# A mixture-of-experts step: x and h turned by VectorE in 32x32 blocks, x in its own column order, down loaded as gate, the bias in one step

## The chip, the cores and the metric

One core of a Trainium2 chip runs the whole program. The metric is the device time of one execution in microseconds, as the median of several runs.

## The reference

One layer of an encoder for 256 prompt frames and 64 sample frames, D_MODEL = 1024, all in float32: one input projection, band attention and a convolution branch, their mix, a LayerNorm, and then a mixture of 32 experts with the best 4 for each frame. The part that matters here is the last:

```python
logits = x @ w_router + b_router
top_val, top_idx = lax.top_k(logits, 4)
gate = softmax(top_val)
# for each frame and each of its 4 experts e
gt = minimum(x @ w_gate[e] + b_gate[e], 7.0)
up = clip(x @ w_up[e] + b_up[e], -7.0, 7.0)
h = gt * sigmoid(1.702 * gt) * (up + 1.0)
y += gate * (h @ w_down[e] + b_down[e])
# then
x = layer_norm(alpha * x + y) * g + b
```

Each expert's w_gate, w_up and w_down has 1024 x 1024 floats (4.19 MB); the 96 matrices are 403 MB.

## The kernel before

The program is written per engine, with semaphores. Ahead of the expert loop stand the projections, attention, convolution, the output projection and the first LayerNorm (`norm1`, `norm1_small`), then the router (`logits`, `largest`, `shares`, `ranked`), which leaves for each frame its rank within each expert and tables with the order of the experts.

**Blocks.** An expert's frames are cut into blocks of 32 slots. All in all there are 58 blocks; the 32 experts, in the order in which they are worked (order comes from `above_at`: one with many frames, then two with few), take 1, 1, 1, 7, 1, 1, 4, 1, 1, 4, 1, 1, 4, 1, 1, 3, 1, 1, 3, 1, 1, 3, 1, 1, 2, 1, 1, 2, 2, 2, 2, 1 blocks here.

**One block on TensorE.** PSUM rows are used as four strips of 32: strip q holds the 32 slots and the columns 256q to 256q + 255. In order: `gate_or_up` for gate (32 steps: 8 chunks of the 1024 inputs by 4 strips, each as two instructions, since float32; then the bias), `combine(i, 0)` of the block before, `gate_or_up` for up, `combine(i, 1)`, `gather` (the next block's rows of x, by the selection matrix `sel`), two transposes of `tin` that turn h, two small matmuls that spread the slot row of the next block (`who`, waited for under `bc_mm`), `combine(i, 2)`, two transposes that turn the gathered x (`turn_x`), and down (32 steps). `combine` sends the finished y of the block before back to the frames: tile 0 and 1 into PSUM banks 4 to 7, tile 2 into banks 4 and 5, and so each waits until VectorE has added what lay there (`yadd`).

**Turning.** Matmuls need x and h with the 1024 inputs on partitions. ScalarE copies the gathered rows from PSUM bank 2 to `tin` (`gathered`), TensorE turns 128 x 128 squares into bank 3, ScalarE copies them to `xg` (`turned`). h is computed by VectorE in `tin`, turned in the same way, and copied to `hT`. For this to give the rows that gate and up expect (partition p holds rows 8p to 8p + 7 of w_gate, 32 KB in one run), LayerNorm writes x in another column order: in `norm1` and `norm1_small` the writes are rearranged from (q c) to (c q), and the router's weights are loaded to match. w_down is loaded as four runs of 8 KB to a partition:

```python
wg_v, wu_v = (w[0].rearrange("e (p c) n -> e p c n", p=P) for w in (w_gate, w_up))
wd_v = w_down[0].rearrange("e (q p j) n -> e p q (j n)", q=Q, j=2)
```

**Bias.** float32 biases are split by GpSimd into three bfloat16 parts, and added by matmuls with a column `hot` that is 1 in the expert's row: high and middle part on 64 rows, low part on 32 rows, four matmuls each.

**VectorE in a block**: clamp of gate, product with ScalarE's sigmoid, `add_tile(i, 0)`, clamp of up, product that makes h, `add_tile(i, 1)`, `add_tile(i, 2)`, gate column and slot masks of the next block.

**Loads.** SP issues gate, up and down of an expert in halves of 2 MB into one of two buffer sets. Each half waits for the matmuls that last read it (`gate_half`, `gate_done`, `up_half`, ...) in the last block of the expert two before. Everything runs through one queue in that order.

Of the kernel before, what the change touches and what calls it, by code (L numbers as in the profile page):

```python
# [14 lines left out]
P = 128  # L15
D = 1024
# [28 lines left out]
def encoder_step(nc, x_prompt, x_sample, cache_k, cache_v, state_conv, w_in, b_in, rel_bias, w_att_o,  # L45
# [8 lines left out]
    def rows(ap):  # L54
        return ap[0].rearrange("(c p) n -> p c n", p=P)
# [3 lines left out]
    wg_v, wu_v = (w[0].rearrange("e (p c) n -> e p c n", p=P) for w in (w_gate, w_up))  # L59
    wd_v = w_down[0].rearrange("e (q p j) n -> e p q (j n)", q=Q, j=2)  # L60
# [8 lines left out]
    with ctx:  # L69
# [4 lines left out]
        SB = ctx.enter_context(nc.sbuf_tensor("SB", [P, S0 + 7902], F32))  # L74
# [70 lines left out]
        raw_hm = view(S0 + 2560, 2, 512)  # L145
        raw_lo = view(S0 + 3584, 2, 256)
# [10 lines left out]
        xg = view(M0 + 256, 2, Q, SLOTS)  # L157
        hT = view(M0 + 512, 2, Q, SLOTS)
        ysb = view(M0 + 768, 256)
        scat = view(M0 + 1024, T)  # L160
        bias_hm = view16(M0 + 1344, BF16, 2, 2, 256)
        bias_lo = view16(M0 + 2522, BF16, 2, 256)
# [4 lines left out]
        rankT = view16(M0 + 2208, F16, T, rows=E)  # L167
        tbl = SB[E:E + 1, M0 + 2208:M0 + 2242].bitcast(I32)
        order = SB[E:E + 1, M0 + 2242:M0 + 2274].bitcast(I32)
        nblk = SB[E:E + 1, M0 + 2274:M0 + 2306].bitcast(I32)  # L170
        tbl3 = SB[E:E + 1, M0 + 2306:M0 + 2322].bitcast(I32)
        sel = view(M0 + 2368, 3, SLOTS)
        hot = view16(M0 + 2464, BF16, 2)
        hot16 = view16(M0 + 2465, F16, 2, rows=E)
        slotno = view(M0 + 2778, 1)
        slotcol = view(M0 + 2466, MAXB)
        slotbase = view(M0 + 2476, MAXB)
        eps_c = view(M0 + 2486, 1)
        gcol = view(M0 + 2487, 3)
        onehot = view(M0 + 2490, E)  # L180
# [79 lines left out]
        def _(sp):  # L260
# [11 lines left out]
            sp.dma_start(bout_bc, b_out.broadcast_to([P, D])).then_inc(sem("bout_in"), 16)  # L272
            for k in range(Q):
                r, c = slice(32 * k, 32 * k + 32), slice(256 * k, 256 * k + 256)
                two = slice(512 * (k // 2), 512 * (k // 2) + 512)
                for which, b in enumerate((b_gate, b_up)):
                    sp.dma_start(raw_hm[r, which, :], b[0, :, two]).then_inc(sem("bias_in"), 16)
                    sp.dma_start(raw_lo[r, which, :], b[0, :, c]).then_inc(sem("bias_in"), 16)
                sp.dma_start(ysb[r, :], b_down[0, :, c]).then_inc(sem("bdown_in"), 16)
# [46 lines left out]
            sp.dma_start(wr, w_router[0].rearrange("(p c) n -> p c n", p=P)).then_inc(sem("wr_in"), 16)  # L326
# [48 lines left out]
        def _(pool):  # L375
# [39 lines left out]
            pool.wait_ge(sem("bias_in"), 256)  # L415
            hm = bias_hm.rearrange("p w h n -> p w (h n)")
            link(pool.tensor_copy(hm, raw_hm))
            link(pool.tensor_tensor(raw_hm, raw_hm, hm, ALU.subtract))
            for r in (slice(32, 64), slice(96, 128)):
                link(pool.tensor_copy(hm[r], raw_hm[r]))  # L420
            for part in range(2):
                link(pool.tensor_copy(bias_lo, raw_lo))
                link(pool.tensor_tensor(raw_lo, raw_lo, bias_lo, ALU.subtract))
            pool.tensor_copy(bias_lo, raw_lo).then_inc(sem("bias_ready"), 1)
# [14 lines left out]
            with pool.Fori(0, E) as k:  # L439
# [3 lines left out]
                with pool.Fori(0, blocks) as b:  # L443
# [32 lines left out]
        def _(act):  # L476
# [125 lines left out]

            def gathered():
                act.copy(tin, PS[:, 2, 0:256]).then_inc(sem("tin_x"), 1)

            def turned():
                act.copy(xg, PS[:, 3, 256:512].rearrange("p (j q s) -> p j q s", j=2, q=Q)).then_inc(sem("xg_ready"), 1)

            act.wait_ge(sem("gath_mm"), 2)
            gathered()  # L610
            act.wait_ge(sem("trx_mm"), 1)
            turned()

            act.wait_ge(sem("tables_done"), 1)
            total = act.value_load(tbl[0:1, E:E + 1], min_val=1, max_val=200)
            with act.Fori(0, total) as i:
                act.wait_ge(sem("gmin"), i + 1)
                act.wait_ge(sem("trx_mm"), i + 1)
                act.activation(tin, PS[:, 0, 0:256], ACT.Sigmoid, scale=SW_ALPHA).then_inc(sem("sig"), 1)  # L619
                act.wait_ge(sem("trh_mm"), i + 1)  # L620
                act.copy(hT, PS[:, 3, 0:256].rearrange("p (j q s) -> p j q s", j=2, q=Q)).then_inc(sem("hT_ready"), 1)  # L621
                act.wait_ge(sem("gath_mm"), i + 3)
                gathered()
                act.wait_ge(sem("trx_mm"), i + 2)
                turned()
                act.wait_ge(sem("down_done"), i + 1)
                act.copy(ysb, PS[:, 2, 256:512]).then_inc(sem("y_sb"), 1)  # L627
# [12 lines left out]
        def _(dve):  # L640
# [149 lines left out]
            def norm1(tt):  # L790
# [6 lines left out]
                for s in range(2):  # L797
# [18 lines left out]
            def norm1_small():  # L816
# [9 lines left out]
                for half in range(2):  # L826
                    k = slice(64 * half, 64 * half + 64)
                    for part in range(2):
                        c = slice(4 * part, 4 * part + 4)
                        ins = dve.scalar_tensor_tensor(  # L830
                            x_part(2, part).rearrange("p (c q) -> p c q", c=4)[:, :, k],
                            v[k].rearrange("p (q c) -> p c q", c=KC)[:, c, :], rstd[k, 2:3],
                            ln1b_half[k].rearrange("p (q c) -> p c q", c=KC)[:, c, :], ALU.mult, ALU.add)
                ins.then_inc(sem("x1_ready"), 1)
# [206 lines left out]
        def _(pe):  # L1041
# [426 lines left out]
```

## Time and profile before

| | us |
|---|---|
| median of 3 runs | 1443.54 (1443.07 to 1443.75) |
| the profiled execution | 1446.62 |
| its span | 1444.9 |
| TensorE busy (matmul) in the span | 1366.1 |
| VectorE busy | 577.5 |
| ScalarE busy | 266.7 |
| GpSimd busy | 115.6 |
| w_gate, w_up, w_down loads | 64 each of 2 MB |

The span is the profiled time from the first to the last instruction; the execution has 1.7 us around it. Busy times of the engines overlap. Matmuls are pipelined, so that in a run of them the start of the next tells the time of one group, not its own duration. The mean granted clock of TensorE was 0.97 of full speed. The DMA moved 459.68 MB, 318 GB/s over the span.

### The profile page before, as it was taken

How to read it: one execution, taken by the hardware profiler on the slowest of the kernel's cores; microseconds unless marked ns; L12 is line 12 of the kernel's file. 1: busy time of each engine (PE TensorE's matmuls, PEld its weight loads, DVE VectorE, ACT ScalarE, POOL GpSimd, SP SyncE). 2: the span in 40 equal slices, each digit the busy share in tenths (PEclk: the TensorE clock that was granted, in tenths of full speed). 3: DMA queues.
4: the chain of work that ended last, by engine and by line, in shares of the span. 5: the costliest groups of instructions: out<-in, count | busy, mean ns of one | idle time of the engine just before them, and what ended most of it. 6: DMA issues, size and time to landing. Idle time of an engine off the chain costs nothing.

```text
span 1444.9 us, 41443 instructions
## 1 busy us (share of the span) xinstructions
PE 1366.1 (95%) x17038; PEld 768.7 (53%) x17039; DVE 577.5 (40%) x1103; ACT 266.7 (18%) x562; POOL 115.6 (8%) x328
## 2 busy tenths in 40 slices
PE   8999999999979999999999999999898999879995
PEld 6777674576544455555555555555454544335552
DVE  0179984551174333333333333333333332313335
ACT  1111113240111211112111211121111111111111
POOL 3400000000001000010001000100000000000000
PEclk9999999999979999999999999999999999989998
DMA  9333333417789960797997997999999999999993
GB/s 302 118 117 116 117 116 127 165 59 281 276 332 410 429 275 0 312 428 319 428 427 321 428 424 321 428 424 428 426 425 427 427 427 424 426 428 427 425 425 110
DMA packets 63794, 459.68 MB, mean 318 GB/s; under 512 B 4562, under 2 KB 7234, under 8 KB 30971
## 3 DMA queue, kind: packets, MB, share of 16 engines
q1 hardware_dynamic: 63482, 459.03, 77.6%
q10 hardware_dynamic: 289, 0.33, 0.1%
q8 instruction: 16, 0.26, 0.1%
q14 instruction: 7, 0.06, 0.0%
HBM read 455.14 MB, written 4.73 MB: 318 GB/s over the span
## 4 chain that ended last, share of the span: by engine, by line
PE 76%; DMA 18%; DVE 2%; SPq 2%; issue 1%; ACT 1%; ACTq 0%; DVEq 0%
PE PS L1354 21%; DMA SB<-in_w_down_dram 17%; PE PS L1063 12%; PE PS L1424 12%; PE PS L1376 6%; PE PS L1335 5%; PE PS L1044 3%; PE PS L1233 3%; PE PS L1174 2%; PE PS L1129 2%; PE PS L1253 2%; SPq L241 2%; PE PS L1082 1%; PE PS L1360 1%; PE PS L1364 1%; PE PS L1089 1%
## 5 line engine op out<-in xcount | busy, mean ns | idle before, releaser
L1354 PE MATMUL PS<-SB 128*32 128x256 f32 x7424 | 439.8, 389 | 31.3 <-DMA SB<-in_w_up_dram 14.8
L1354 PEld LDWEIGHTS PS<-SB 128*32 128x32 f32 x7424 | 238.9, 112 | 216.0 <-issue 60.2
L958 DVE SCALAR_TENSOR_TENSOR SB<-PS,SB 128x1024 f32<-128x1024 f32 x176 | 193.7, 1100 | 80.9 <-PE PS L1376 80.7
L1424 PE MATMUL PS<-SB 128*32 128x256 f32 x3712 | 214.2, 381 | 9.0 <-DMA SB<-in_w_down_dram 9.0
L968 DVE TENSOR_SCALAR PS<-PS 128x256 f32<-128x256 f32 x58 | 25.1, 433 | 383.7 <-PE PS L1364 383.7
L1063 PE MATMUL PS<-SB 128*128 128x320 f32 x640 | 172.7, 432 | 0.0
L1424 PEld LDWEIGHTS PS<-SB 128*32 128x32 f32 x3712 | 113.7, 110 | 91.4 <-DMA SB<-in_w_down_dram 13.6
L1063 PEld LDWEIGHTS PS<-SB 128*128 128x128 f32 x640 | 121.4, 190 | 50.4
L1376 PE MATMUL PS<-SB 32*128 32x256 f32 (+1 forms) x1416 | 124.0, 420 | 1.5 <-DVE SB L958 1.0
L688 DVE SCALAR_TENSOR_TENSOR SB<-SB 128x350 f32<-128x350 f32 x240 | 118.6, 573 | 0.0
L1335 PE MATMUL PS<-SB 128*32 128x256 f32 (+1 forms) x1416 | 97.9, 390 | 0.0
L621 ACT COPY SB<-PS 128x256 f32<-128x256 f32 x58 | 21.6, 372 | 399.3 <-PE PS L1044 399.3
L975 DVE TENSOR_SCALAR PS<-PS 128x256 f32<-128x256 f32 x58 | 25.1, 433 | 151.1 <-PE PS L1364 151.1
L1044 PE MATMUL PS<-SB 128*128 128x128 f32 (+6 forms) x390 | 75.6, 303 | 7.6 <-DMA SB<-in_x_prompt_dram 4.4
L1044 PEld LDWEIGHTS PS<-SB 128*128 128x128 f32 (+6 forms) x390 | 47.4, 160 | 58.4 <-issue 31.1
L619 ACT ACT_TABLE_LOAD x58 | 74.4, 1283 | 1.6 <-issue 0.6
L462 POOL CAST SB<-SB 128x1 bf16 x58 | 10.9, 187 | 779.5 <-PE PS L1414 779.5
L1335 PEld LDWEIGHTS PS<-SB 128*32 128x32 f32 (+1 forms) x1416 | 34.0, 108 | 54.5 <-issue 44.4
L1376 PEld LDWEIGHTS PS<-SB 32*128 32x128 f32 (+1 forms) x1416 | 49.5, 166 | 24.2 <-issue 1.5
L627 ACT COPY SB<-PS 128x256 f32<-128x256 f32 x58 | 21.6, 372 | 199.2 <-PE PS L1424 199.2
L619 ACT ACTIVATE SB<-PS 128x256 f32<-128x256 f32 x58 | 22.3, 384 | 182.0 <-DVE PS L968 182.0
L493 ACT ACTIVATE SB<-PS,SB 128x320 f32 x40 | 21.1, 528 | 141.1 <-PE PS L1063 141.0
(228 smaller groups left out, 957.2 us busy)
## 6 DMA issues: line engine op xcount, KB each, us to landing
SB<-in_w_gate_dram SPq DMA_DIRECT2D x64, 2048.0 KB, 27.4
SB<-in_w_up_dram SPq DMA_DIRECT2D x64, 2048.0 KB, 32.7
SB<-in_w_down_dram SPq DMA_DIRECT2D x64, 2048.0 KB, 34.6
SB<-in_w_in_dram SPq DMA_DIRECT2D x13, 2048.0 KB, 7.9
SB<-in_w_pw_dram SPq DMA_DIRECT2D x2, 2048.0 KB, 9.9
SB<-in_w_att_o_dram SPq DMA_DIRECT2D x2, 2048.0 KB, 7.9
SB<-in_w_out_dram SPq DMA_DIRECT2D x2, 2048.0 KB, 8.2
SB<-in_w_in_dram SPq DMA_DIRECT2D x4, 512.0 KB, 9.6
```

Of the source, the lines that this page charges most:

```text
L241: eng.dma_start(buf[:, 4 * h:4 * h + 4, :], src[:, step * h:step * h + step, :]).then_inc(sem(f"{name}_{h}"), 16)
L619: act.activation(tin, PS[:, 0, 0:256], ACT.Sigmoid, scale=SW_ALPHA).then_inc(sem("sig"), 1)
L688: dve.scalar_tensor_tensor(yc[:, c, :], uext[:, c, bass.ds(k, CONVN)], dwT[:, c, bass.ds(k, 1)], yc[:, c, :], ALU.mult, ALU.add).then_inc( ...
L958: dve.scalar_tensor_tensor(y, ps, gcol[:, tt:tt + 1], y, ALU.mult, ALU.add).then_inc(sem("yadd"), 1)
L1044: return pe.transpose(out, in_, ident[0:k, 0:k])
L1063: ins = pe.matmul(PS[:, t, 0:T], ring[s][:, c, P * t:P * t + P], xT[:, c, :], start=(c == 0), stop=(c == KC - 1))
L1129: ins = pe.matmul(PS[:, 2 * s + tt, :], xT[:, c, t0:t0 + r], ring[s][:, c, :], start=(c == 0), stop=(c == KC - 1))
L1233: ins = pe.matmul(PS[:, t % 4, 0:T], ring[s][:, c, P * (t % 4):P * (t % 4) + P], oT[:, c, :], start=(c == 0), stop=(c == KC - 1))
L1335: ins = pe.matmul(PS[32 * q:32 * q + 32, 2, 0:256], sel[r, tt, :], x_part(tt, q // 2)[:, k], start=(tt == 0), stop=(tt == 2))
L1354: ins = pe.matmul(PS[32 * q:32 * q + 32, bank, 0:256], xg[:, c % 2, c // 2, :], buf[:, c, 256 * q:256 * q + 256], start=(c == 0), stop=False)
L1376: ins = pe.matmul(out, scat[r, TT[tt][0]:sum(TT[tt])], ysb[r, :], start=True, stop=True)
L1424: ins = pe.matmul(PS[32 * n:32 * n + 32, 2, 256:512], hT[:, ck % 2, ck // 2, :], WD[par][:, ck, 256 * n:256 * n + 256], start=(ck == 0), s ...
```

## The change

VectorE transposes x and h in 32 x 32 blocks straight from where they are: x from PSUM bank 3, where `gather` now writes, to `xg`; h from `tin` to `hT`. It reads every eighth column (`by_chunk`), so that partition 32q + b gets the inputs 256q + 8b + c: rows 8p + c, the order of the weights. The transposes of TensorE and three copies of ScalarE go. x keeps its column order from LayerNorm on; w_router is loaded by `rows`, the scaling of x into `yacc` is one operation, and w_down is loaded as w_gate. The three parts of the bias lie on rows 0 to 31, 32 to 63 and 64 to 95 and are added by four matmuls of 96 rows; the tables and the float16 ranks move to partitions 96 to 127. GpSimd's split is done in pieces of 32 rows.

```diff
-    wg_v, wu_v = (w[0].rearrange("e (p c) n -> e p c n", p=P) for w in (w_gate, w_up))
-    wd_v = w_down[0].rearrange("e (q p j) n -> e p q (j n)", q=Q, j=2)
+    wg_v, wu_v, wd_v = (w[0].rearrange("e (p c) n -> e p c n", p=P) for w in (w_gate, w_up, w_down))
...
         def by_chunk(row):
 
-            return row.rearrange("p (q c) -> p q c", c=KC)
+            return row.rearrange("p (b c) -> p c b", c=KC)
...
+            for part in range(3):
+                for which, b in enumerate((b_gate, b_up)):
+                    sp.dma_start(raw[32 * part:32 * part + 32, which, :], b[0]).then_inc(sem("bias_in"), 16)
...
-            sp.dma_start(wr, w_router[0].rearrange("(p c) n -> p c n", p=P)).then_inc(sem("wr_in"), 16)
+            sp.dma_start(wr, rows(w_router)).then_inc(sem("wr_in"), 16)
...
+            pool.wait_ge(sem("bias_in"), 96)
+            for which in range(2):
+                tab = bias[which].rearrange("p q n -> p (q n)")
+                for part in range(3):
+                    for k in range(part, 3):
+                        r = slice(32 * k, 32 * k + 32)
+                        link(pool.tensor_copy(tab[r], raw[r, which, :]))
+                        if k > part:
+                            link(pool.tensor_tensor(raw[r, which, :], raw[r, which, :], tab[r], ALU.subtract))
...
                     pool.wait_ge(sem("bc_mm"), i + 1)
+                    pool.wait_ge(sem("sel_ready"), i + 2)
...
-                act.wait_ge(sem("trx_mm"), i + 1)
+                act.wait_ge(sem("hT_ready"), i + 1)
                 act.activation(tin, PS[:, 0, 0:256], ACT.Sigmoid, scale=SW_ALPHA).then_inc(sem("sig"), 1)
-                act.wait_ge(sem("trh_mm"), i + 1)
-                act.copy(hT, PS[:, 3, 0:256].rearrange("p (j q s) -> p j q s", j=2, q=Q)).then_inc(sem("hT_ready"), 1)
-                act.wait_ge(sem("gath_mm"), i + 3)
-                gathered()
-                act.wait_ge(sem("trx_mm"), i + 2)
-                turned()
...
-                dve.scalar_tensor_tensor(xs[:, D * tt:D * tt + D].rearrange("p (c q) -> p c q", c=KC),
-                                         v.rearrange("p (q c) -> p c q", c=KC), rstd[:, tt:tt + 1],
-                                         ln1b_bc.rearrange("p (q c) -> p c q", c=KC), ALU.mult, ALU.add).then_inc(sem("x1_ready"), 1)
+                dve.scalar_tensor_tensor(xs[:, D * tt:D * tt + D], v, rstd[:, tt:tt + 1], ln1b_bc, ALU.mult, ALU.add)\
+                   .then_inc(sem("x1_ready"), 1)
...
+            def turn_x():
+
+                dve.transpose(xg, by_chunk(PS[:, 3, 0:256])).then_inc(sem("xg_ready"), 1)
...
+                    dve.wait_ge(sem("h_ready"), i + 2)
+                    dve.transpose(hT, by_chunk(tin)).then_inc(sem("hT_ready"), 1)
+
                     add_tile(i, 1)
+
+                    dve.wait_ge(sem("gath_mm"), i + 3)
+                    turn_x()
+
                     add_tile(i, 2)
...
                 for q in range(Q):
-                    r = slice(64 * (q // 2), 64 * (q // 2) + 64)
-                    pe.matmul(PS[32 * q:32 * q + 32, bank, 0:256], hot[r, 0:1].broadcast_to([64, SLOTS]), bias_hm[r, which, q % 2, :],
-                              start=False, stop=False)
-                for q in range(Q):
-                    r = slice(32 * q, 32 * q + 32)
-                    ins = pe.matmul(PS[r, bank, 0:256], hot[r, 0:1].broadcast_to([32, SLOTS]), bias_lo[r, which, :],
+                    ins = pe.matmul(PS[32 * q:32 * q + 32, bank, 0:256], hot[:, 0:1].broadcast_to([96, SLOTS]), bias[which][:, q, :],
                                     start=False, stop=True)
```

TensorE, in the loop body, from the bias of up to down. Before:
```order
L1360 MATMUL PS<-SB 32x256 x4
L1364 MATMUL PS<-SB 32x256 x4
L1400 REGISTER_ALU
L1376 MATMUL PS<-SB 128x256 x4
L1402 REGISTER_ALU
L1335 MATMUL PS<-SB 32x256 x12
L1407 REGISTER_ALU
L1044 MATMUL PS<-SB 128x128 x2
L1413 MATMUL PS<-SB 128x256
L1414 MATMUL PS<-SB 128x64
L1415 REGISTER_ALU
L1376 MATMUL PS<-SB 64x256 x4
L1044 MATMUL PS<-SB 128x128 x2
L1424 MATMUL PS<-SB 32x256 x32
```
The change:
```order
L1324 MATMUL PS<-SB 32x256 x4
L1359 REGISTER_ALU
L1336 MATMUL PS<-SB 128x256 x4
L1361 REGISTER_ALU
L1307 MATMUL PS<-SB 32x256 x12
L1364 REGISTER_ALU
L1366 MATMUL PS<-SB 128x256
L1367 MATMUL PS<-SB 128x64
L1368 REGISTER_ALU
L1336 MATMUL PS<-SB 64x256 x4
L1376 MATMUL PS<-SB 32x256 x32
```
One bias group of the two is gone (L1360 and L1364 are L1324 now), and both pairs of 128x128 transposes (L1044); the rest follows in the old order.

VectorE, in the loop body, from the clamp of up to the add of the third tile. Before:
```order
L975 TENSOR_SCALAR PS<-PS 128x256
L976 REGISTER_ALU
L978 SCALAR_TENSOR_TENSOR SB<-PS,SB 128x256
L951 REGISTER_ALU
L958 SCALAR_TENSOR_TENSOR SB<-PS,SB 128x1024
L951 REGISTER_ALU
L958 SCALAR_TENSOR_TENSOR SB<-PS,SB 128x512
```
The change:
```order
L940 TENSOR_SCALAR PS<-PS 128x256
L941 REGISTER_ALU
L943 SCALAR_TENSOR_TENSOR SB<-PS,SB 128x256
L946 STREAM_TRANSPOSE SB<-SB 128x256
L916 REGISTER_ALU
L923 SCALAR_TENSOR_TENSOR SB<-PS,SB 128x1024
L950 REGISTER_ALU
L905 STREAM_TRANSPOSE SB<-PS 128x256
L916 REGISTER_ALU
L923 SCALAR_TENSOR_TENSOR SB<-PS,SB 128x512
```
The transpose of h (L946) stands between the product that makes h and the add of tile 1, and the transpose of x (L905) between the adds of tiles 1 and 2.

## Rows read from the trace of the kernel before

**Rows 1.** The page's head.
```profile
span 1444.9 us, 41443 instructions
```

**Rows 2.** Windows: stretch and its length, busy of each engine, PEclk, DMA share, GB/s.
```profile
435.00:445.00 10.00, 10.00 (x128) 4.99 (x132) 4.17 (x8) 1.48 (x2) 2.80 (x8) 0.72 0.96 376
530.00:586.00 56.00, 56.00 (x920) 29.67 (x916) 19.62 (x35) 11.86 (x23) 5.83 (x20) 1.00 0.00 1
670.00:690.00 20.00, 20.00 (x338) 10.63 (x334) 7.30 (x12) 3.40 (x7) 1.45 (x5) 1.00 0.60 236
...
866.00:886.00 20.00, 20.00 (x334) 10.55 (x330) 7.41 (x14) 3.06 (x6) 1.45 (x5) 1.00 0.59 236
890.00:1390.00 500.00, 465.46 (x7325) 238.74 (x7321) 158.65 (x279) 85.48 (x168) 40.72 (x140) 0.97 1.01 426
```

**Rows 3.** Two load starts on the queue SP, and groups by line between.
```profile
586.13 2.49 SPq L241 DMA_DIRECT2D SB<-in_w_gate_dram  x2
...
683.47 2.49 SPq L241 DMA_DIRECT2D SB<-in_w_gate_dram  x2
...
L968 DVE TENSOR_SCALAR PS<-PS 128x256 f32<-128x256 f32 x6 | 2.6, 432 | 37.6 <-PE PS L1364 37.6
```

**Rows 4.** Timeline of TensorE in one block: start, duration.
```profile
624.91 0.29 PE L1360 MATMUL PS<-SB 64*32 64x256 bf16 x4
625.13 0.29 PE L1364 MATMUL PS<-SB 32*32 32x256 bf16 x4
625.34 0.71 PE L1376 MATMUL PS<-SB 32*128 32x256 f32 x8
625.99 1.64 PE L1335 MATMUL PS<-SB 128*32 128x256 f32 x24
627.56 0.51 PE L1044 MATMUL PS<-SB 128*128 128x128 f32 x2
627.99 0.28 PE L1413 MATMUL PS<-SB 32*128 32x256 f16 x1
...
628.23 0.66 PE L1376 MATMUL PS<-SB 32*64 32x256 f32 x8
628.82 0.44 PE L1044 MATMUL PS<-SB 128*128 128x128 f32 x2
629.19 3.66 PE L1424 MATMUL PS<-SB 128*32 128x256 f32 x64
```

**Rows 5.** Timeline of VectorE in the same block.
```profile
625.47 0.43 DVE L975 TENSOR_SCALAR PS<-PS 128x256 f32<-128x256 f32 x1 [2.17 <-PE PS L1364]
626.01 0.42 DVE L978 SCALAR_TENSOR_TENSOR SB<-PS,SB 128x256 f32<-128x256 f32 x1
626.35 1.28 DVE L958 SCALAR_TENSOR_TENSOR SB<-PS,SB 128x1024 f32<-128x1024 f32 x1
```

**Rows 6.** Timeline of TensorE at three waits for a load.
```profile
502.26 1.93 PE L1424 MATMUL PS<-SB 128*32 128x256 f32 x32 [1.24 <-DMA SB<-in_w_down_dram]
...
1274.52 3.64 PE L1354 MATMUL PS<-SB 128*32 128x256 f32 x32 [1.83 <-DMA SB<-in_w_gate_dram]
...
1294.17 1.93 PE L1424 MATMUL PS<-SB 128*32 128x256 f32 x32 [1.86 <-DMA SB<-in_w_down_dram]
```

**Rows 7.** Timeline of VectorE in the first LayerNorm of the small tile.
```profile
410.16 0.75 DVE L824 SCALAR_TENSOR_TENSOR SB<-SB 128x512 f32<-128x512 f32 x1
...
411.44 2.73 DVE L830 SCALAR_TENSOR_TENSOR SB<-SB 64x256 f32<-64x256 f32 x4
```

**Rows 8.** Windows of a down load alone and of gate and up alone.
```profile
930.00:939.00 9.00, 9.00 (x146) 4.54 (x138) 5.17 (x9) 1.02 (x3) 1.45 (x5) 1.00 1.01 422
941.00:957.00 16.00, 16.00 (x270) 8.45 (x266) 5.69 (x10) 3.06 (x6) 0.85 (x4) 1.00 1.01 429
```

**Rows 9.** Timeline of GpSimd at the bias split and after it.
```profile
43.06 2.13 POOL L418 TENSOR_TENSOR SB<-SB 128x1024 f32<-128x1024 f32 x1
...
427.35 0.35 POOL L434 TENSOR_TENSOR SB<-SB 128x96 f32<-128x96 f32 x1 [374.69 <-DVE SB L904]
```

More of the change, by code:

```diff
@@ L143, in encoder_step @@
         st_rows = view(5 * WB + 2560 + P + D, D, rows=HALO)
[L145 to L146 removed]
+        raw = view(S0 + 2560, 2, D, rows=96)
         bout_bc = view(S0, D)
@@ L156, in encoder_step @@
         tin = view(M0, 256)
-        xg = view(M0 + 256, 2, Q, SLOTS)
-        hT = view(M0 + 512, 2, Q, SLOTS)
+        xg = view(M0 + 256, KC, SLOTS)
+        hT = view(M0 + 512, KC, SLOTS)
         ysb = view(M0 + 768, 256)
         scat = view(M0 + 1024, T)
-        bias_hm = view16(M0 + 1344, BF16, 2, 2, 256)
-        bias_lo = view16(M0 + 2522, BF16, 2, 256)
+        bias = [view16(M0 + o, BF16, Q, 256, rows=96) for o in (1344, 2362)]
         ident = view(M0 + 1856, P)
@@ L166, in encoder_step @@
         rank = view(M0 + 2112, 3, E)
[L167 to L180, printed above, removed]
+        low = slice(96, 128)
+        rankT = SB[low, M0 + 1344:M0 + 1504].bitcast(F16)
+        tbl = SB[96:97, M0 + 1504:M0 + 1538].bitcast(I32)
+        order = SB[96:97, M0 + 1538:M0 + 1570].bitcast(I32)
+        nblk = SB[96:97, M0 + 1570:M0 + 1602].bitcast(I32)
+        tbl3 = SB[96:97, M0 + 1602:M0 + 1618].bitcast(I32)
+        sel = view(M0 + 2208, 3, SLOTS)
+        hot = view16(M0 + 2304, BF16, 2, rows=96)
+        hot16 = SB[low, M0 + 2305:M0 + 2306].bitcast(F16)
+        slotno = view(M0 + 2874, 1)
+        slotcol = view(M0 + 2306, MAXB)
+        slotbase = view(M0 + 2316, MAXB)
+        eps_c = view(M0 + 2326, 1)
+        gcol = view(M0 + 2327, 3)
+        onehot = view(M0 + 2330, E)
         wr = view(M0 + 512, KC, E)
@@ L272, in _ @@
             sp.dma_start(bout_bc, b_out.broadcast_to([P, D])).then_inc(sem("bout_in"), 16)
+            for part in range(3):
+                for which, b in enumerate((b_gate, b_up)):
+                    sp.dma_start(raw[32 * part:32 * part + 32, which, :], b[0]).then_inc(sem("bias_in"), 16)
             for k in range(Q):
[L274 to L279, printed above, removed]
+                sp.dma_start(ysb[32 * k:32 * k + 32, :], b_down[0, :, 256 * k:256 * k + 256]).then_inc(sem("bdown_in"), 16)
             def group(s, src, user, count):
@@ L413, in _ @@
                 pool.wait_ge(sem("xr_ready"), tt + 1)
[L415 to L424, printed above, removed]
+            pool.wait_ge(sem("bias_in"), 96)
[7 more added lines that the diff above has]
+                            link(pool.tensor_tensor(raw[r, which, :], raw[r, which, :], tab[r], ALU.subtract))
+            pool.sem_inc(sem("bias_ready"), 1)
             pool.wait_ge(sem("bias_ready"), 1)
@@ L825, in norm1_small @@
                 unit(2, P)
[L826 to L834, printed above, removed]
+                dve.scalar_tensor_tensor(xs[:, 2 * D:2560], v, rstd[:, 2:3], ln1b_half, ALU.mult, ALU.add).then_inc(sem("x1_ready"), 1)
             for tt in range(2):
```

47 lines of the change are left out of this document (10 added, 37 removed).

## The prediction

> **What bounds the kernel now.** The page's head [rows 1] gives the span, 1444.9 us; the profiled execution itself took 1446.62 us, 3.1 us more than the median of the runs shown, 1443.54 us. I make the sum against the profiled execution and take it off both. The first 434 us are mixing, first norm and router; the expert loop runs from 434.9 to 1425.5 us, so I read it by windows first [rows 2]. While the loop works, two things take turns. In 530 to 586 us the DMA moves nothing and TensorE is busy for the whole 56.00 us: the expert there has seven blocks, both buffer sets are full, and the next load waits until a block ends. Three smaller gaps of the same sort follow, each at the end of an expert with four blocks; the first is 20 us x (1 - 0.60) = 8.0 us, the last 8.2. From 890 us on the DMA is busy without a break at 426 GB/s (4.19 MB in 9.85 us, 29.5 us for the three matrices of an expert) and TensorE waits for it now and then. The last such wait is the down wait that ends at 1294.17 [rows 6]; eight more blocks follow with none.
>
> So TensorE time saved is worth something only where TensorE holds the DMA up (before 886 us) or where the DMA no longer holds TensorE up (after 1294). Between two starts of a load after a gap there are six blocks and 97.34 us [rows 3], 16.2 us for a block; the three experts loaded in that time cost 88.5 us of DMA. The gap is the difference, and it is the only slack of the DMA in that round.
>
> **TensorE's block.** The timeline of one block [rows 4] is gapless from the end of up's bias; by start to start, 625.34 to 629.19 is 3.85 us = combine 0.65, gather 1.57, turning h 0.43, the slot-row broadcast 0.24, third combine 0.59, turning x 0.37.
> - Bias: two sets of four matmuls, 64 and 32 rows (0.22 and 0.21 us), become one set of four on 96 rows. Both sets cost the same though the rows differ, so I take 0.22 for the new one: 0.22 saved for gate and 0.22 for up, 0.44 in a block. If 96 rows cost two sets, nothing is saved; this end is kept.
> - The four TensorE transposes go: 0.43 + 0.37 = 0.80 us.
> - ScalarE loses three copies. They were beside other work; what they waited for is gone too.
> - What comes in place stands on VectorE's path [rows 5]. With U the time at which up is done (625.34), the clamp starts at U + 0.13, the last product of h at U + 0.67 and ends at U + 1.09; the add of the second combine starts at U + 1.01 and ends at U + 2.29. The third combine writes the same PSUM banks and TensorE comes to it at U + 2.89, 0.60 late enough. In the change the transpose of h stands ahead of that add. It waits for the product (0.11 us, as the product waited for the clamp), so it runs from U + 1.20 to U + 1.20 + X; the add ends at U + 2.40 + X, and the combine can start some 0.06 us later, at U + 2.46 + X. TensorE, with no transposes, comes there at U + 0.65 + 1.57 + 0.24 = U + 2.46. It will wait for X, whatever X is.
>
> The saving in a block is then s = 0.44 + 0.80 - X = 1.24 - X. The down matmuls need the transposed h at U + 3.05 + X; it is there. The transpose of x from PSUM comes behind the add, beside the third combine and the down matmuls (3.6 us), and costs nothing; the slot masks that close VectorE's block then move back by X and stay ahead of the next gate, which has all 3.6 us of the down matmuls before it.
>
> **X** has no row. From below, the clamp of 128x256 takes 0.43 us [rows 5] from PSUM, contiguous. From above, the strided LayerNorm step [rows 7]: 4 of 64x256 in 2.73 us, 0.68 each, while the contiguous 128x512 took 0.75. It reads SBUF with a step of eight floats as the transpose of h will (by_chunk), and has the same 256 elements. I take 0.68 and s = 0.56; the ends are 0.37 (half of the contiguous 0.75, s = 0.87) and some 1.0 (s = 0.2, also what a bias step without saving gives). The Trainium skill, SBUF — State Buffer, on SBUF "cachelines", says that an access which crosses to a new 16-byte line pays a penalty, free only up to four fp32; by that rule the step of eight pays on every element, and the row agrees, 0.68 against 0.37.
>
> **The DMA.** Down is loaded in runs of 32 KB a partition where it was four of 8 KB. By windows, a stretch in which the queue moved only down ran at 422 GB/s, one with gate and up alone at 429 [rows 8]. 4.19 MB then take 9.78 for 9.94 us, and I take the difference, 0.17 us (rounded up) a matrix. Zero is the other end. The loads of biases are six for sixteen, the same bytes; the router weights (now rows of 32 floats) are loaded well ahead of their use. Both hidden.
>
> **Ahead of the loop.** The strided norm steps go (2.73 to about 0.75 for the last), the router chain ends 2 us sooner and the first gather saves a copy and two transposes. But the first experts' loads are in a queue that is already busy. Only the hole in 435 to 445, 10 x (1 - 376/426) = 1.2 us, can close: 1.2 us gained of 2.7. GpSimd's bias split grows to twelve casts and six subtractions of 1024 columns, 12 x 1.1 + 6 x 2.2 = 26 us near 50 us, and its queue has nothing else to do until 427 us [rows 9]. Its new waits in the loop are for its own earlier steps, which are done by then.
>
> **The sum.**
> - Up to the end of the first gap: hole 1.2, three downs 0.5, and the blocks between the seven-block expert's down, which came late and will (1.24 us wait [rows 6]), and its last gate: five blocks, 5s.
> - Each of three rounds: the first down of the four-block expert is fed by six matrices behind the gap, 59 us. TensorE is at the second half of that down one block after the down of [rows 4], at 629.19 + 16.2 + 1.8 - 586.13 = 61 us behind the gap, about when they land. The 3s won before it goes into a wait, save some 0.5 us of slack; two blocks behind it count: 2s + 0.5, and two downs 0.34. Three times: 6s + 2.5.
> - 886 to 1294, no gap: 14 downs, 2.4 us. TensorE's saving there is all given back.
> - 1294 on: eight blocks, 8s. The last experts' loads keep pace up to s of about 1.2.
> - After the loop nothing changes.
> Together 6.6 + 19s. For s = 0.56 that is 17.2 us. Waits grow, and with them the risk of the halved clock: 32 matmuls that took 1.93 us after a wait of 1.86 took 3.64 after one of 1.83 that came behind other waits [rows 6]. I take off 1 us for one such half matrix. **16.2 us less: 1446.62 to 1430.4, and 1443.54 to 1427.3.**
>
> **Rivals.**
> 1. The transposes run at one element a cycle whatever the step: X about 0.45, s = 0.79, 6.6 + 15.0 - 1 = 20.6, 1423. For: the clamp row. Against: the strided row. The Trainium skill, VectorE: DVE Perf Modes, "The three transpose paths", lists 311 ns for 128x128 bf16; by it a VectorE transpose is cheap, and no run here shows one yet. Chance 0.28.
> 2. Waits take more back: loads of e.g. up are late too, every longer wait halves the clock, or 96 rows cost as much as before (s = 0.12). Then 6.6 + 2.3 = 9, 1434.5. For: TensorE is just in time at every first down of a round. Chance 0.14.
> 3. **Slower.** A transpose is done block by block with a fixed cost each. The fixed part of a VectorE operation is some 0.15 us by [rows 5] (0.43 for 256 columns, 1.28 for 1024). Eight 32x32 blocks at 0.15 are 1.2, with 0.5 to read at the strided rate 1.7: s = -0.46. Where TensorE leads, 25 blocks to 886 us and the last eight, that costs 15.2 us, less 4 of DMA and start: +11, 1454.5. It decides from X = 1.24 + 4/33 = 1.36. For: nothing in the trace shows this operation. Against: the other 256-element operations all lie at 0.42 to 0.68. Chance 0.09.
> 4. X near 1.3, or the change does not shorten what it says: the saving of TensorE is eaten by its own new wait; 1443, within 0.2%. Chance 0.04.
>
> **How the numbers follow.** The forecast (X 0.6 to 0.75) has 0.45. Faster takes it with rivals 1 and 2: 0.87; same 0.04; slower 0.09. The measurement of this kernel can tell some 0.2%, 2.9 us. The range takes in s = 0.87 with no clock loss (6.6 + 16.5 = 23, 1420.4, and 2 more for the DMA term at 0.2) and s = 0.12 with no DMA gain (about 5.5, 1438): 1418.5 to 1437.
>
> **What would show it.** Right: TensorE idle before the third combine, released by VectorE's add, near X in each block; blocks of 15.4 us where no load is late; the first gap ended near 581.5; down stretches at 428 GB/s; waits for up and down in every round before 886. Wrong: a transpose over 1.2 us; TensorE late to the third combine without waiting; the DMA with gaps after 890 us; bias sets of 0.4 us.

## The result and the profile after

| | kernel before | the change |
|---|---|---|
| median (lowest to highest) of 4 runs | 1443.30 us (1440.02 to 1443.75) | 1423.31 us (1421.14 to 1424.31) |
| ratio | | 0.9864, 95% interval 0.9845 to 0.9883 |
| the profiled execution, its span | 1446.62, 1444.9 | 1423.89, 1422.2 |

The change is 20.0 us faster by the medians. 16.2 us were forecast (1427.3), and 1423.3 lies in the range of 1418.5 to 1437. The two profiled executions differ by 22.7 us.

The page of the kernel after: head, busy times, granted clock in 40 slices, and the groups of the gate and up matmuls and of the transpose of h.

```profile
span 1422.2 us, 40006 instructions
...
PE 1287.2 (91%) x16340; PEld 729.5 (51%) x16341; DVE 636.8 (45%) x1210; ACT 206.5 (15%) x386; POOL 135.0 (9%) x337
...
PEclk9999999999979999999999999999999999899998
...
L1319 PE MATMUL PS<-SB 128*32 128x256 f32 x7424 | 442.7, 390 | 56.9 <-DMA SB<-in_w_up_dram 26.7
...
L946 DVE STREAM_TRANSPOSE SB<-SB 128x256 f32<-128x256 f32 x58 | 37.7, 650 | 2.0
```

X, the time of the transpose of h, for which no row stood, is 0.65 us. The windows of [rows 2], of the kernel after:

```profile
435.00:445.00 10.00, 9.54 (x166) 4.98 (x166) 6.24 (x11) 0.29 (x1) 1.85 (x6) 1.00 1.00 422
530.00:586.00 56.00, 54.13 (x928) 28.52 (x924) 25.25 (x45) 7.30 (x11) 4.92 (x17) 1.00 0.16 63
...
890.00:1390.00 500.00, 435.38 (x7113) 224.97 (x7109) 188.24 (x340) 58.74 (x86) 42.76 (x141) 0.97 1.01 428
```

The hole behind the router is closed (422 for 376 GB/s), TensorE has idle time in every block now (54.13 busy of 56.00), and behind 890 us the DMA moves 428 for 426 GB/s.

The first load behind each gap on SP's queue, of the kernel after ([rows 3] before), and the group of VectorE's clamp of gate between the first two:

```profile
576.24 2.14 SPq L239 DMA_DIRECT2D SB<-in_w_gate_dram  x2
...
673.02 2.15 SPq L239 DMA_DIRECT2D SB<-in_w_gate_dram  x2
...
768.37 2.14 SPq L239 DMA_DIRECT2D SB<-in_w_gate_dram  x2
...
L933 DVE TENSOR_SCALAR PS<-PS 128x256 f32<-128x256 f32 x6 | 2.6, 432 | 37.6 <-PE PS L1324 37.6
```

Still six blocks a round, and 96.78 us for the first (97.34 before) and 95.35 us for the second.

One block of TensorE after, against [rows 4] (start, duration, in brackets the idle time before it and what ended it):

```profile
609.31 3.66 PE L1319 MATMUL PS<-SB 128*32 128x256 f32 x64
612.78 0.29 PE L1324 MATMUL PS<-SB 96*32 96x256 bf16 x4
613.01 0.71 PE L1336 MATMUL PS<-SB 32*128 32x256 f32 x8
613.65 1.64 PE L1307 MATMUL PS<-SB 128*32 128x256 f32 x24
615.22 0.28 PE L1366 MATMUL PS<-SB 32*128 32x256 f16 x1
615.34 0.19 PE L1367 MATMUL PS<-SB 32*128 32x64 f16 x1
616.00 0.66 PE L1336 MATMUL PS<-SB 32*64 32x256 f32 x8 [0.47 <-DVE SB L923]
616.59 3.66 PE L1376 MATMUL PS<-SB 128*32 128x256 f32 x64
```

VectorE beside it, against [rows 5]:

```profile
613.12 0.43 DVE L940 TENSOR_SCALAR PS<-PS 128x256 f32<-128x256 f32 x1 [1.85 <-PE PS L1324]
613.66 0.42 DVE L943 SCALAR_TENSOR_TENSOR SB<-PS,SB 128x256 f32<-128x256 f32 x1
614.12 0.65 DVE L946 STREAM_TRANSPOSE SB<-SB 128x256 f32<-128x256 f32 x1
614.70 1.24 DVE L923 SCALAR_TENSOR_TENSOR SB<-PS,SB 128x1024 f32<-128x1024 f32 x1
615.86 0.44 DVE L905 STREAM_TRANSPOSE SB<-PS 128x256 f32<-128x256 f32 x1
616.73 0.75 DVE L923 SCALAR_TENSOR_TENSOR SB<-PS,SB 128x512 f32<-128x512 f32 x1 [0.43 <-PE PS L1336]
```

With U = 613.01, TensorE has nothing to do from about U + 2.5, the add ends at U + 2.93 and the third combine starts at U + 2.99, 0.10 later than before. The new wait is there in every block: 27.1 us in 57 waits. The transpose of x ends (616.30) before the down matmuls begin, and nothing waits for it, as forecast. By the starts of the clamp of gate, blocks without a late load come every 15.08 us, where it was 16.00: s, the saving in a block, is 0.92, not 0.56.

A window ahead of the loop, of the kernel before:

```profile
270.00:280.00 10.00, 8.26 (x51) 5.80 (x50) 6.76 (x18) 4.93 (x19) 0.00 (x0) 0.84 0.12 48
330.00:340.00 10.00, 8.28 (x43) 5.89 (x42) 0.49 (x1) 1.54 (x4) 0.00 (x0) 0.83 0.90 336
```

In the profiled execution of the kernel before TensorE's clock was at its lower level for a while in each of these (0.84 and 0.83 of full), in that of the kernel after in neither (1.00, 1.00). Runs below have one, both or none. The matmuls of the output projection start at 373.38 before and at 370.19 after. Ahead of them only the loads of the biases and GpSimd's split changed, and in the profiles of the ten runs below that share this part with the change the same start lies anywhere from 368.69 to 373.58. So I take these 3.2 us as chance; they are about what the profiles differ by more than the medians.

### The profile page after: what moved, and what is told of

Same layout as the page of the kernel before. It is cut to its first block, busy times and chain, and to the rows that moved or that the text cites. A ratio compares the mean times of both kernels' runs of the same rounds, so it can differ in the third digit from the quotient of the medians.

```text
span 1422.2 us, 40006 instructions
## 1 busy us (share of the span) xinstructions
PE 1287.2 (91%) x16340; PEld 729.5 (51%) x16341; DVE 636.8 (45%) x1210; ACT 206.5 (15%) x386; POOL 135.0 (9%) x337
## 4 chain that ended last, share of the span: by engine, by line
PE 63%; DMA 24%; DVE 8%; issue 3%; ACT 1%; another core or an unknown queue 0%; SPq 0%; DVEq 0%; POOLq 0%; POOL 0%; ACTq 0%
DMA SB<-in_w_down_dram 20%; PE PS L1319 20%; PE PS L1035 12%; PE PS L1376 11%; PE PS L1336 4%; DVE SB L923 4%; DMA SB<-in_w_up_dram 3%; PE PS L1205 2%; PE PS L1146 2%; PE PS L1101 2%; PE PS L1225 2%; PE PS L1054 1%; DVE PS L940 1%; DVE SB L943 1%; PE PS L1061 1%
## 5 line engine op out<-in xcount | busy, mean ns | idle before, releaser
L1035 PE MATMUL PS<-SB 128*128 128x320 f32 x640 | 172.7, 432 | 0.0
L1336 PE MATMUL PS<-SB 32*128 32x256 f32 (+1 forms) x1416 | 123.8, 420 | 27.8 <-DVE SB L923 27.1
L607 ACT COPY SB<-PS 128x256 f32<-128x256 f32 x58 | 21.6, 372 | 680.7 <-PE PS L1376 680.7
L459 POOL CAST SB<-SB 96x1 bf16 x58 | 10.6, 183 | 743.4 <-PE PS L1367 743.3
L946 DVE STREAM_TRANSPOSE SB<-SB 128x256 f32<-128x256 f32 x58 | 37.7, 650 | 2.0
L1146 PE MATMUL PS<-SB 128*128 128x320 f32 x128 | 38.0, 440 | 0.0
L935 DVE TENSOR_TENSOR SB<-SB,PS 128x256 f32<-128x256 f32 x58 | 24.5, 422 | 26.1 <-ACT SB L605 26.1
```

The costliest lines, as they stand in the source:

```text
L946: dve.transpose(hT, by_chunk(tin)).then_inc(sem("hT_ready"), 1)
L1035: ins = pe.matmul(PS[:, t, 0:T], ring[s][:, c, P * t:P * t + P], xT[:, c, :], start=(c == 0), stop=(c == KC - 1))
L1146: ins = pe.matmul(PS[:, 6 + j % 2, 0:T], ring[s][:, c, P * t:P * t + P], zc[:, c, :], start=(c == 0), stop=(c == KC - 1))
L1336: ins = pe.matmul(out, scat[r, TT[tt][0]:sum(TT[tt])], ysb[r, :], start=True, stop=True)
```

## The experiments

All times are in us; the ratio is to the kernel before, run beside each on the same chip. The block is the distance of two starts of the clamp of gate where no load is late.

| run | median | ratio [95%] | block |
|---|---|---|---|
| the change, again | 1424.39 | 0.9869 [0.9847, 0.9890] | 15.08 |
| transpose of h behind the add | 1411.52 | 0.9782 [0.9764, 0.9801] | 14.54 |
| w_down in runs of 8 KB | 1427.19 | 0.9889 [0.9870, 0.9908] | 15.08 |
| bias in two sets | 1434.54 | 0.9943 [0.9925, 0.9961] | 15.74 |
| h turned twice | 1433.57 | 0.9930 [0.9910, 0.9949] | 15.75 |
| x turned twice | 1423.68 | 0.9861 [0.9841, 0.9880] | 15.08 |
| before, with the bias part alone | 1435.62 | 0.9944 [0.9925, 0.9964] | 15.35 |
| bias set on 64 rows | 1423.13 (one run) | | 15.30 |
| turning alone | 1438.11 | 0.9953 [0.9938, 0.9968] | 15.74 |
| norm step three times more | 1424.32 | 0.9863 [0.9844, 0.9882] | 15.08 |
| h turned without a step | 1418.58 | 0.9826 [0.9803, 0.9849] | 14.87 |

The theory: the gain is TensorE's shorter block where TensorE leads, and X is in it in full, because the add that the third combine waits for stands behind the transpose. The rival: loads and the start made the gain, and the block's parts are hidden.

**The change again.**

> The change itself, beside the experiments of this call, so that each can be held against it on the same chip. Both theories: about 1423.3 us, 20 us below the kernel before (ratio 0.986), blocks of 15.1 us between 530 and 600 us, third combine waiting some 0.47 us for VectorE.

It came out so, within 1.1 us. The four runs that hold the change's block (this one, the result, and the two below that added hidden work) give 0.9861 to 0.9869.

**The transpose of h behind the add.**

```diff
+                    add_tile(i, 1)
                     dve.wait_ge(sem("h_ready"), i + 2)
                     dve.transpose(hT, by_chunk(tin)).then_inc(sem("hT_ready"), 1)
-                    add_tile(i, 1)
```

> The change with the transpose of h put behind the add of the second combine. My theory (the block is TensorE's, and X costs it through the add that stands behind the transpose): the third combine starts without its wait of 0.47 us, the block falls from 15.08 to about 14.6 us, the transposed h comes at about U + 3.0, just ahead of the down matmuls at U + 3.1. The tail of eight blocks gains 8 x 0.47 = 3.8 us if the last loads keep pace, the blocks ahead of the gaps some 2 to 4 more, and longer waits for loads take part of it: 1416 to 1420 us. Rival A: the down matmuls then wait for h instead, by 0.3 us or more: 1421 to 1424. Rival B: the saving of the change did not come from the block but from loads and start alone: no difference, 1423.3.

12.9 us faster than the change, more than any theory said. VectorE and TensorE in one block of this run:

```profile
609.06 1.28 DVE L923 SCALAR_TENSOR_TENSOR SB<-PS,SB 128x1024 f32<-128x1024 f32 x1
610.25 0.62 DVE L948 STREAM_TRANSPOSE SB<-SB 128x256 f32<-128x256 f32 x1
...
610.39 0.19 PE L1367 MATMUL PS<-SB 32*128 32x64 f16 x1
610.51 0.66 PE L1336 MATMUL PS<-SB 32*64 32x256 f32 x8
...
611.10 3.66 PE L1376 MATMUL PS<-SB 128*32 128x256 f32 x64
```

The third combine starts with no wait at all and the turned h is there (610.87) 0.2 us before the down matmuls. The block loses 0.54 us: the 0.47 of the wait and 0.07 beside it. So the whole price of X came from its place ahead of the add. By the prediction's 19 blocks 0.54 us are worth 10.3. From the starts of the clamp of gate in the two profiles, the three rounds alone gave 5.0 where 6 x 0.54 = 3.2 were due. Behind the down wait of the third round the change run again took 3.53 us for 32 matmuls (829.87), this run 1.93 (823.32): the lower clock was missing there. This kernel beats both others: 0.9782, 31 us less than before.

**w_down in four runs of 8 KB.** The rows of w_down do not belong to the elements of h beside them here.

```diff
-    wg_v, wu_v, wd_v = (w[0].rearrange("e (p c) n -> e p c n", p=P) for w in (w_gate, w_up, w_down))
+    wg_v, wu_v = (w[0].rearrange("e (p c) n -> e p c n", p=P) for w in (w_gate, w_up))
+    wd_v = w_down[0].rearrange("e (q p j) n -> e p q (j n)", q=Q, j=2)
```

> The change with w_down loaded in four runs of 8 KB a partition, as before, everything else as in the change; the rows of w_down then do not stand beside the elements of h that they belong to, so that product is taken with permuted rows. My theory (24 of the 32 downs lie where the DMA sets the time, 0.17 us each by the windows): 4 us slower than the change, 1427 (1426 to 1429), DMA at 426 instead of 429 GB/s in the stretch behind 890 us. By the packets of the two traces (314 ns for 8 KB, 614.6 for 16 KB) a down takes 2 % longer, 0.2 us, 5 us in all. Rival: the DMA was not the bound there, TensorE's blocks were: no difference.

2.8 us slower by the medians (1427.19 where 1427 was expected), with intervals that overlap; the time alone would settle little. The trace settles it. Starts of the clamp of gate, nine experts apart in the stretch where the DMA never rests; first of the kernel before, then of the change, then of this run:

```profile
1034.31 0.43 DVE L968 TENSOR_SCALAR PS<-PS 128x256 f32<-128x256 f32 x1 [8.10 <-PE PS L1364]
...
1300.04 0.43 DVE L968 TENSOR_SCALAR PS<-PS 128x256 f32<-128x256 f32 x1 [8.11 <-PE PS L1364]
```

```profile
1020.00 0.43 DVE L933 TENSOR_SCALAR PS<-PS 128x256 f32<-128x256 f32 x1 [7.84 <-PE PS L1324]
...
1284.32 0.43 DVE L933 TENSOR_SCALAR PS<-PS 128x256 f32<-128x256 f32 x1 [6.56 <-PE PS L1324]
```

```profile
1021.85 0.43 DVE L934 TENSOR_SCALAR PS<-PS 128x256 f32<-128x256 f32 x1 [8.00 <-PE PS L1325]
...
1287.56 0.43 DVE L934 TENSOR_SCALAR PS<-PS 128x256 f32<-128x256 f32 x1 [8.01 <-PE PS L1325]
```

265.73, 264.32 and 265.71 us: the kernel before and this run agree to 0.02, the change needs 1.4 us less for nine experts, 0.16 us for each down. The run with two bias sets, whose block is longer by 0.66 us, needs 264.28 (1022.65 to 1286.93): no saving of TensorE counts there.

**The bias in two sets.**

```diff
-                for q in range(Q):
-                    ins = pe.matmul(PS[32 * q:32 * q + 32, bank, 0:256], hot[:, 0:1].broadcast_to([96, SLOTS]),
-                                    bias[which][:, q, :], start=False, stop=True)
+                for rows_, last in ((slice(0, 64), False), (slice(64, 96), True)):
+                    k = rows_.stop - rows_.start
+                    for q in range(Q):
+                        ins = pe.matmul(PS[32 * q:32 * q + 32, bank, 0:256], hot[rows_, 0:1].broadcast_to([k, SLOTS]),
+                                        bias[which][rows_, q, :], start=False, stop=last)
```

> The change with the bias added in two sets again, 64 and 32 rows, from the same 96 rows of parts. If a set costs only its own 0.22 us (the price in the prediction), the block grows by 0.44 us and the whole by at most 19 x 0.44 = 8 us: 1431 at most. If the second set costs TensorE 0.32 us, as the starts of the two traces say (gate to first combine 4.03 before, 3.71 now), the block grows by 0.65 us to 15.7 and the whole by up to 12 us, 1433 to 1435. If 32 rows behind 64 alone bring the extra, the block shows it here too. Rival: the bias is hidden and the block grows by less than 0.2 us.

The block grows by 0.66 us and the whole by 10 us, as the second case had it. A second set costs 0.33, one and a half times its own duration. One gate of this run:

```profile
608.06 3.64 PE L1319 MATMUL PS<-SB 128*32 128x256 f32 x64
611.63 0.51 PE L1326 MATMUL PS<-SB 64*32 64x256 bf16 x8
612.07 0.71 PE L1338 MATMUL PS<-SB 32*128 32x256 f32 x8
```

The two sets take 0.44 (611.63 to 612.07), so 0.22 of it is the second set; the rest is ahead of the bias: 3.57 us from the gate's start, 3.47 in the block above (609.31 to 612.78).

**The set on 64 rows**, to see where that comes from.

```diff
-                    ins = pe.matmul(PS[32 * q:32 * q + 32, bank, 0:256], hot[:, 0:1].broadcast_to([96, SLOTS]), bias[which][:, q, :],
+                    ins = pe.matmul(PS[32 * q:32 * q + 32, bank, 0:256], hot[0:64, 0:1].broadcast_to([64, SLOTS]), bias[which][0:64, q, :],
```

> The change with the one set of bias matmuls on 64 rows instead of 96; it leaves out the low third of the split biases. If the extra 0.11 us of a set comes from the second set, the block stays at 15.08 us. If it comes from the change of rows from 128 to 64 in front of it (the gate matmuls took 3.59 us up to a set of 64 rows and 3.48 up to one of 96), the block grows by 0.22 us to 15.3 and the distance from the gate's start to the bias by 0.11.

```profile
605.11 3.64 PE L1319 MATMUL PS<-SB 128*32 128x256 f32 x64
608.67 0.29 PE L1324 MATMUL PS<-SB 64*32 64x256 bf16 x4
608.89 0.71 PE L1336 MATMUL PS<-SB 32*128 32x256 f32 x8
```

3.56 us up to the bias, a block of 15.30: the extra 0.1 us is there with 64 rows and no second set. Why four matmuls on 64 rows start later behind those on 128 rows than four on 96 rows do stays open. Its time is that of one run and can say nothing of 0.2 us a block.

**The bias part alone.** The kernel before with the three parts on 96 rows, six loads and one set; the diff is the bias part of the change.

> The kernel before with the bias part of the change alone: six loads, parts on 96 rows, one set of four matmuls. With 0.33 us for a set (the run with two sets: its block is 0.66 us longer) the block falls from 16.00 to 15.34 us; by the same proportion as there (10 us for 0.66) the whole falls to 1431 to 1434. With 0.22 us for a set, as the prediction had it, 15.56 and 1435 to 1437. Rival: the gain of one set needs the turning on VectorE too: less than 3 us.

The block is 15.35 us, as expected with 0.33 us for a set and not the 15.56 of 0.22. The time is not as expected: 8.1 us faster by the ratio (0.0056 x 1443), 1435.62, which lies outside 1431 to 1434 and in the range given for 0.22 us. Taken out of the change the same part costs 10 to 11. Whether it is worth less here is not shown, since the intervals of the two (3 us each way) overlap. The rival, under 3 us, is out.

**h turned twice**, one transpose behind the other.

```diff
+                    dve.transpose(hT, by_chunk(tin)).then_inc(sem("hT_first"), 1)
+                    dve.wait_ge(sem("hT_first"), i + 1)
                     dve.transpose(hT, by_chunk(tin)).then_inc(sem("hT_ready"), 1)
```

> The change with the transpose of h done twice, one behind the other (the second waits for the first), so that X is 0.65 + 0.11 + 0.65 = 1.4 us. My theory (all of X stands on TensorE's path through the add): the third combine waits 1.2 instead of 0.47 us, the block takes 15.8 instead of 15.08 us. By the starts of the blocks of the two runs with the quicker block and the one with two bias sets (12.6 us for 0.54, 7 to 10 us for 0.66 a block) the whole is 10 to 14 us slower than the change, 1433 to 1438. It is also the test of the point where the slower rival of the prediction decides (X = 1.36, equal to the kernel before): by it this kernel comes to 1444; by the measured s (0.92 at X = 0.65) it is still some 6 us quicker than before. Rival: VectorE has slack there, under 3 us.

```profile
607.38 0.66 PE L1338 MATMUL PS<-SB 32*64 32x256 f32 x8 [1.15 <-DVE SB L923]
```

The wait grows from 0.47 to 1.15 us and the block by 0.67: what the second transpose adds on VectorE appears on TensorE in full. The whole grows by about 9, a little less than the 10 to 14 expected. With X at 1.32 the kernel is still 0.7% (10 us) faster than before. By the measured s the block would be level with the old one at X = 0.65 + 0.92 = 1.57, not at the 1.24 of the prediction.

**x turned twice**, the extra one into an unused part of bank 3.

```diff
+                dve.transpose(PS[:, 3, 256:512].rearrange("p (c b) -> p c b", c=KC), by_chunk(PS[:, 3, 0:256]))
                 dve.transpose(xg, by_chunk(PS[:, 3, 0:256])).then_inc(sem("xg_ready"), 1)
```

> The change with one more transpose of the gathered x (0.44 us, from PSUM into an unused part of bank 3) ahead of the real one. My theory: this transpose stands beside the third combine and the down matmuls and costs nothing, 1423 to 1424.5; only the first block of the loop may start 0.4 us later. Rival: the masks and the third add behind it are on the path, the block grows by 0.4 us and the whole by 8 us.

Block 15.08, ratio 0.9861: the same kind of instruction, one place further down, is free, as expected.

**h turned without a step.** Neighbouring columns make a 32x32 block, so the down product meets other rows of w_down than it should.

```diff
-                    dve.transpose(hT, by_chunk(tin)).then_inc(sem("hT_ready"), 1)
+                    dve.transpose(hT.rearrange("p c s -> p (c s)"), tin).then_inc(sem("hT_ready"), 1)
```

> The change with the transpose of h read without a step: 32 neighbouring columns make a block, instead of every eighth column. The down product then meets permuted rows of w_down; all else is as it was. It asks what the step of eight floats in SBUF costs. The transpose of x, from PSUM with the same step, took 0.44 us, that of h from SBUF 0.65. If the step is what costs in SBUF, X falls to 0.42 to 0.45, the third combine waits 0.26 instead of 0.47, the block takes 14.87 and the whole is 3 to 5 us faster than the change, 1418 to 1421. That would be the time of the prediction's first rival. If SBUF or the transpose itself costs it, X stays 0.65 and the time 1423 to 1424.5.

Groups by line of this run, 500 to 1390 us, then the same two of the change:

```profile
L946 DVE STREAM_TRANSPOSE SB<-SB 128x256 f32<-128x256 f32 x53 | 23.6, 445 | 1.8
L905 DVE STREAM_TRANSPOSE SB<-PS 128x256 f32<-128x256 f32 x53 | 23.1, 436 | 0.6 <-PE PS L1307 0.6
```

```profile
L946 DVE STREAM_TRANSPOSE SB<-SB 128x256 f32<-128x256 f32 x53 | 34.5, 650 | 1.8
...
L905 DVE STREAM_TRANSPOSE SB<-PS 128x256 f32<-128x256 f32 x53 | 23.4, 441 | 0.0
```

The step of eight costs 0.205 us of 0.65 when SBUF is read. From PSUM the transpose takes 0.44 with the step, as long as the one from SBUF without it; one from PSUM without a step was not run. The third combine of this run:

```profile
617.66 0.66 PE L1336 MATMUL PS<-SB 32*64 32x256 f32 x8 [0.26 <-DVE SB L923]
```

The wait falls to 0.26 and the block to 14.87, as expected; the whole is 5 to 6 us faster than the change, by its two measurements, where 3 to 5 were expected. The Trainium skill, SBUF — State Buffer, on SBUF "cachelines", has a penalty for each new 16-byte line; the run agrees that there is one for SBUF, and gives its size on a transpose: 650 for 445 ns.

**The turning alone:** two bias sets and w_down in four runs (permuted rows again), both diffs as above.

> The turning on VectorE alone: the change with the bias in two sets (64 and 32 rows) and w_down in four runs of 8 KB a partition; the product with w_down is taken with permuted rows again. What is left of the change is X against the four TensorE transposes, the combine behind it, and the shorter start. Block 15.74 us, 0.26 less than before. If the parts add up (of 20 us the bias took 8.6 to 10.2 and down 2.8 in the runs so far), 7 to 8.5 us faster than before, 1435 to 1437. Rival: the parts overlap (each one's saving goes into the same waits), then this alone gives over 9 us or under 5.

6.8 us faster than before (0.0047 x 1443), just under the 7 to 8.5 of adding up, and not the under 5 or over 9 of the rival. With 8.1 to 11 for the bias and about 3 for down that makes 18 to 21, for the 19.6 of the whole. The parts add up as far as intervals of 2 to 3 us can tell.

**The norm step three times more.**

```diff
+                for _ in range(3):
+                    link(dve.scalar_tensor_tensor(xs[:, 2 * D:2560], v, rstd[:, 2:3], ln1b_half, ALU.mult, ALU.add))
                 dve.scalar_tensor_tensor(xs[:, 2 * D:2560], v, rstd[:, 2:3], ln1b_half, ALU.mult, ALU.add).then_inc(sem("x1_ready"), 1)
```

> The change with the last LayerNorm step of the small tile written four times, each waiting for the one before, some 2.8 us more in the chain to the router, more than the 2.0 us that the change took out of it. If only the 1.2 us hole of the DMA behind the router is worth anything, as the prediction had it, 0.5 to 1.3 us slower than the change, 1424 to 1425. Rival A: the whole chain counts up to the first gap and stays: 2.8 us, 1426. Rival B: nothing counts, the queue of loads is full: within 0.5 us.

The first block started 2.25 us later than in the change run again, the first load behind the gap 1.50 later (578.10 for 576.60), and the time is the same: 1424.32 for 1424.39. The 1.5 us go between 630 and 645 us. TensorE at the down wait of the first round, in the profile of the change and in that of this run:

```profile
637.32 2.90 PE L1376 MATMUL PS<-SB 128*32 128x256 f32 x32 [2.29 <-DMA SB<-in_w_down_dram]
639.97 4.42 PE L1319 MATMUL PS<-SB 128*32 128x256 f32 x64
```

```profile
639.42 1.93 PE L1378 MATMUL PS<-SB 128*32 128x256 f32 x32 [2.29 <-DMA SB<-in_w_down_dram]
641.17 3.64 PE L1321 MATMUL PS<-SB 128*32 128x256 f32 x64
```

The same wait of 2.29 us, and behind it 2.90 and 4.42 us of matmuls in the one, 1.93 and 3.64 in the other: the lower clock cost the change 1.7 us here and this run nothing. The change run again and the run with x turned twice had the lower clock here too. What decides it is not shown. So the trace does not say that the start is worth nothing, only that 1.5 us of it are less than what one wait may or may not cost. The time fits both 0.5 to 1.3 us and rival B, and which of them holds was not settled.

## Why the prediction was right, by its steps

The profiles' 22.7 us against the terms of the sum, read from the starts of the clamp of gate in both traces (before and after: 588.13 and 577.91 at the first gap, 880.39 and 866.76 at the last, 1300.04 and 1284.32 behind the last late load):

| term | forecast | measured |
|---|---|---|
| chance ahead of the loop | | 3.2 |
| start and first gap | 4.5 | 7.0 |
| three rounds | 5.9 | 3.4 |
| 886 to 1294 us | 2.4 | 2.1 |
| tail, eight blocks | 4.5 | 7.0 |
| one lower clock | -1.0 | in the rounds |
| sum (forecast: before rounding) | 16.2 | 22.7 |

- **X.** "I take 0.68" from the strided norm step: 0.65. The step was the reason, as taken; the run without it gives 0.445, the 0.45 of rival 1. That rival fell, though its time (1423) was met: had one gone by the time alone, it would have been taken for right.
- **The wait.** The mechanism was right. That the third combine "will wait for X, whatever X is" held in both directions: 0.26 us idle at X = 0.45, 0.47 at 0.65, 1.15 with two. It started at U + 2.99 where U + 2.46 + 0.65 = 3.11 was worked out: the transpose began 0.04 and not 0.11 us behind the product, and the add 0.07 us before the transpose's end. The turning thus gave 3.85 - 3.58 = 0.27 us a block (start of the combine to start of down) and not 0.12.
- **Bias: the term that was mis-sized.** "0.22 saved for gate and 0.22 for up": it was 0.32 to 0.33 each, 0.65 in a block. The step priced a set by its own duration and did not look at what stands ahead of it. [Rows 4] begins at the bias and could not show it. With 0.27 this makes s = 0.92.
- **Start and first gap.** 5s was right in form: 5 x 0.92 = 4.6, and 2.4 for the rest where 1.7 was taken. "The first gap ended near 581.5": it ended at 576.24; of the 5.3 us between, 3.2 are the chance ahead of the loop. GpSimd's split took 27 us (42.46 to 69.2) where 26 were forecast, and is hidden.
- **Rounds.** "The 3s won before it goes into a wait" held: in the three rounds there are waits for down of 2.29 to 2.31 us, and for up ahead of them (0.57, 1.48 and 0.67). By 6s + 2.5 the rounds should have given 8.0 at s = 0.92, and they gave 3.4. About 3.2 of what is missing is the clock: behind the first and the third of these waits it was at its lower level, 1.7 and 1.5 us; "one such half matrix", 1 us, was too few. About 1.4 is the slack. The "some 0.5 us of slack" of each round was not there: TensorE was already at the limit in the kernel before. TensorE at the down wait of the second round, before and after, and of the third, after:

```profile
745.02 1.93 PE L1424 MATMUL PS<-SB 128*32 128x256 f32 x32 [0.56 <-DMA SB<-in_w_down_dram]
```

```profile
734.34 1.93 PE L1376 MATMUL PS<-SB 128*32 128x256 f32 x32 [2.31 <-DMA SB<-in_w_down_dram]
...
829.53 3.47 PE L1376 MATMUL PS<-SB 128*32 128x256 f32 x32 [2.30 <-DMA SB<-in_w_down_dram]
```

In the kernel before that half begins 61.55 us behind the load at 683.47, in the change 61.32 behind that at 673.02. In the first and third round it is 61.5 and 61.6 before (the next gate starts 1.75 us behind it) and 61.1 and 61.2 after. The earlier landing thus gave 0.2 to 0.5 us a round, where 0.5 + 0.34 were put down.
- **The stretch without a gap.** 14 x 0.17 = 2.4: measured 2.1, and 0.16 for a down in the nine experts above. This is the best step of the prediction; it came from two windows of 9 and 16 us.
- **Tail.** 8s gives 7.4 with s = 0.92; 7.0 measured.
- **Rivals.** Of rival 2, "96 rows cost as much as before" is out: a set on 96 rows takes 0.23 (612.78 to 613.01). Its other half was there in part, the waits for up and the lower clock in the rounds, but took 3 us and not 8. 3 and 4 are out by X, and the run with h turned twice shows that even X = 1.32 is faster than before. The upper end of the range, 1437, does not fit its own sum, 1438; nothing hangs on it.

So the time was right to 4 us partly by luck, since errors took each other back. The saving of a block was too small by 0.36 us (6.8 us by 19s) and the start by 0.7. Against that stand a clock loss too small by about 2 us, the slack that was not there (1.4), and 0.3 to 0.4 each in the stretch without a gap and in the tail.

## What to carry to other kernels

When work moves to an idle engine, its price is decided by what it is put in front of there. 0.65 us of VectorE cost 0.54 a block (0.47 of it a plain wait) ahead of an add that TensorE waits for, and nothing one place later; swapping two lines was worth over half as much as the whole change. And read the price of a small step as the distance between the starts of its neighbours with and without it, not as its own duration.

## What was not expected of the hardware

- Four bf16 bias matmuls on 64 rows, behind float32 matmuls on 128 rows, begin 0.1 us later than four on 96 rows (3.56 and 3.57 us from the gate's start, 3.47 with 96).
- A transpose on VectorE of 128x256 float32, in 32x32 blocks, takes 0.44 us from PSUM with a step of eight floats, 0.445 from SBUF without and 0.65 with it.
- Equal waits need not have equal consequences: behind 2.29 us of waiting TensorE ran at the lower clock in the profile of the change and not in that with the norm step three times more.
